# Two-layer decoder step on one core: norm sums, weight loads and cache copies moved at the start, at the layer boundary and ahead of the output projection

## The reference, cut to what matters

```python
def layer(x, lp):                       # 256 prompt tokens and 8 x 4 sample tokens, D = 1024, float32
    xn = rms(x, g_mix)
    q, k, v, xb, gb, gc, cu, cv = split(xn @ w_in)
    ya = dilated window attention of 3 groups of 2 heads (q, k RMS-normed, shared position bias;
         samples attend to the caches), groups weighed by their softmax denominators
    yb = gb * conv3(gc * xb)
    yc = gelu(cu) * (tril(c_ws) @ rms(gelu(cv)) + c_bs)
    h = x + concat(ya, yb, yc) @ w_out
    return h + peer(rms(h, g_ffn))

def peer(xn, wq, k1, k2, eu, ev):       # 8 heads, 16384 experts, top 16 of each head
    q = xn @ wq                          # per head two halves
    e, g = product_key_top16(q, k1, k2)  # 128 expert numbers and gates a token
    hid = gelu(einsum('nd,nhkd->nhk', xn, eu[e]))
    return einsum('nhk,nhkd->nd', g * hid, ev[e])
```

## Time and profile before

| | |
|---|---|
| median of 3 runs | 1879.64 us (1879.1 to 1884.08) |
| profiled execution | 1883.43 us |
| its span, first to last instruction | 1881.7 us |
| busy: PE, DVE, ACT, POOL | 1597.1, 1108.8, 593.0, 681.3 us |
| DMA | 729.73 MB, mean 388 GB/s; q0 (gathers and the caches' loads) 627.43 MB, q1 (SP) 100.48 MB |
| first gather of layer 0 and 1 issued | 222.20 and 1134.31 us |
| mean granted TensorE clock | 0.955 |

### The profile page before, as it was taken

The page is one execution under the profiler, slowest core; times in us unless marked ns, Lnnn a source line. Parts: engine busy times, 40 slices in busy tenths (PEclk is TensorE's granted clock), DMA queues, the critical chain, the costliest instruction groups (busy, mean ns, idle before and its releaser), DMA issues.

```text
span 1881.7 us, 18470 instructions
## 1 busy us (share of the span) xinstructions
PE 1597.1 (85%) x5856; PEld 854.3 (45%) x5856; DVE 1108.8 (59%) x2766; ACT 593.0 (32%) x1854; POOL 681.3 (36%) x672
## 2 busy tenths in 40 slices
PE   6979989998787878777799999999898788777776
PEld 4758955454333333223137897554443333322221
DVE  2233475767877875444444436757778777644444
ACT  2223233333333332222233323323333333322222
POOL 2130134445454534334321103544444544443331
PEclk8889999999899989999999999999998988999999
DMA  5697799999999999999969988999999999999996
GB/s 173 265 395 293 288 379 422 421 421 421 421 421 421 422 421 421 421 422 421 422 251 370 370 332 336 420 421 421 421 421 421 422 421 421 421 422 421 422 421 265
DMA packets 102488, 729.73 MB, mean 388 GB/s; under 512 B 14827, under 2 KB 15925, under 8 KB 21624
## 3 DMA queue, kind: packets, MB, share of 16 engines
q0 software_dynamic: 90112, 627.43, 80.8%
q1 hardware_dynamic: 11732, 100.48, 13.6%
q10 hardware_dynamic: 548, 0.65, 0.1%
HBM read 724.25 MB, written 48.10 MB: 410 GB/s over the span
## 4 chain that ended last, share of the span: by engine, by line
DMA 45%; PE 37%; DVE 10%; ACT 2%; issue 2%; DVEq 1%; POOL 1%; ACTq 1%; SPq 0%; POOLq 0%
DMA arena<-peer_uv,idx 22%; PE bank L1659 18%; DMA wring<-peer_uv,idx 8%; DMA qf<-peer_uv,idx 8%; PE bank L1425 5%; PE bank L1592 4%; PE bank L1623 3%; PE bank L1420 3%; DVE arena L1259 3%; DMA yt<-peer_uv,idx 2%; DMA arena<-cache_keys 2%; DMA arena<-w_out 1%; DVE wring L1259 1%; ACT diag L822 1%; POOL arena L614 1%
## 5 line engine op out<-in xcount | busy, mean ns | idle before, releaser
L1659 PE MATMUL bank<-arena,diag 128*128 128x512 f32 (+1 forms) x1464 | 708.7, 628 | 156.4 <-ACT diag L822 156.2
L614 POOL DMA_INDIRECT arena<-peer_uv,idx x366 | 398.0, 1088 | 654.6 <-PE bank L1659 494.8
L1259 DVE SCALAR_TENSOR_TENSOR arena<-arena,xn 128x1024 f32<-128x1024 f32 x366 | 442.8, 1224 | 295.6 <-DMA arena<-peer_uv,idx 294.1
L1659 PEld LDWEIGHTS bank<-arena,diag 128*128 128x128 f32 (+1 forms) x1464 | 268.4, 190 | 552.4 <-issue 313.1
L814 ACT ACTIVATE act<-hid 128x2 f32<-128x2 f32 x288 | 58.5, 203 | 907.7 <-DVE arena L1259 593.4
L1659 PE MATMUL bank<-wring,diag 128*128 128x512 f32 (+1 forms) x384 | 191.0, 621 | 41.7 <-ACT diag L822 41.7
L822 ACT ACTIVATE diag<-ident,weight 128x128 f32<-128x128 f32 (+1 forms) x576 | 194.7, 385 | 20.1 <-issue 0.3
L1259 DVE SCALAR_TENSOR_TENSOR wring<-wring,xn 128x1024 f32<-128x1024 f32 x96 | 117.4, 1223 | 77.9 <-DMA wring<-peer_uv,idx 76.8
L614 POOL DMA_INDIRECT wring<-peer_uv,idx x96 | 99.3, 1035 | 156.5 <-PE bank L1659 153.1
L817 ACT ACTIVATE weight<-act,gate 128x1 f32<-128x1 f32 x576 | 138.6, 287 | 21.0 <-issue 1.4
L1659 PE MATMUL bank<-qf,diag 128*128 128x512 f32 (+1 forms) x248 | 117.4, 613 | 25.1 <-ACT diag L822 25.1
(11 more groups left out here) (260 smaller groups left out, 1524.0 us busy)
## 6 DMA issues: line engine op xcount, KB each, us to landing
kvs<-cache_a_kv_w SPq DMA_DIRECT2D x32, 1022.0 KB, 10.8
wring<-w_col SPq DMA_DIRECT2D x16, 1024.0 KB, 8.0
wring<-w_tok SPq DMA_DIRECT2D x8, 1408.0 KB, 11.1
arena<-peer_wq SPq DMA_DIRECT2D x10, 1024.0 KB, 20.6
kvs<-cache_a_kv_w SPq DMA_DIRECT2D x16, 508.0 KB, 11.2
arena<-peer_uv,idx POOLq DMA_INDIRECT x366, 21.3
qf<-cache_keys POOLq DMA_DIRECT2D x8, 576.0 KB, 10.4
qf<-cache_values POOLq DMA_DIRECT2D x8, 576.0 KB, 12.2
```

Source lines behind the costliest of these rows:

```text
L614: pool.indirect_dma_start(out=ring[j], out_offset=None, in_=io["peer_uv"], in_offset=bass.IndirectOffsetOnAxis(ap=idx[:, n:n + 1], axis=0) ...
L1259: last = v.scalar_tensor_tensor(out=ring[j][:, 0:D], in0=ring[j][:, 0:D], scalar=1.0, in1=xn[:, i, :], op0=ALU.mult, op1=ALU.mult, accum_o ...
L1659: last = pe.matmul(bank[b0 + half][0:r, :], diag[:, n % 16, 0:r], ring[SLOT_OF[n]][:, D + 512 * half:D + 512 * half + 512], start=False, s ...
```

## The change

- `ms_bank`: the mean of tile 1 goes to bank 3 (before: 1).
- The gains have a semaphore of their own; ACT waits for two loads only and ahead of that does one activation that brings in the square-root table; DVE waits for the gains before its first scaling. In layer 0, PE waits for tile 0 before A0, for tile 1 before A1, and for tile 2 where it did before, ahead of q0.
- Eight shift copies of layer 1 (m = 0 to 7) are issued after SP's small loads, once the first square is done. In layer 1 the copies 8 to 16 follow, one after each of nine loads, then 17 to 23 as before.
- The third quarter of w_out goes to ring slot 4 and is issued ahead of the second, once probt_ps has counted the layer's last transposes of probabilities; query chunk 3, which uses slot 4 later, is issued after 4 and 5, once h_ps has reached 14. Slot 1's first gather does not wait for h_ps. The wait for rows_out stands ahead of query chunk 1.
- `BEFORE_W` is 72: slots 9 and 10 are used up to column 208 in both layers, 11 slots serve the last columns, and layer 1's first two loads are issued from there. A0 and B0 of layer 1 are interleaved with groups 114 to 129, one step k in each.

```diff
-BEFORE_W = 24
+BEFORE_W = 72
...
+        gain_loaded = sem("gain_loaded")
...
-            return bank[(2, 1, 7)[i]]
+            return bank[(2, 3, 7)[i]]
...
-            return (wring[:, 0, 0:KCH * PAIR], ring[0], ring[1], wring[:, 1, 0:KCH * PAIR])[chunk]
+            return (wring[:, 0, 0:KCH * PAIR], ring[0], ring[4], wring[:, 1, 0:KCH * PAIR])[chunk]
...
-            sp.dma_start(gains[:, :, :], io["gain_cols"]).then_inc(x_loaded, 16)
+            sp.dma_start(gains[:, :, :], io["gain_cols"]).then_inc(gain_loaded, 16)
...
+            sp.wait_ge(sq_done, 1)
+            for m in range(8):
+                shift(1, m)
             for l in range(DEPTH):
...
                     load_w(l, c)
-                    for m in range(3 * (c - 2) // 2, 3 * (c - 1) // 2 if c < N_IN else 17):
-                        shift(l, m)
+                    if l == 0:
+                        for m in range(3 * (c - 2) // 2, 3 * (c - 1) // 2 if c < N_IN else 17):
+                            shift(l, m)
+                    elif c < N_IN - 1:
+                        shift(l, c + 6)
+                sp.wait_ge(probt_ps, 3 * (l + 1))
+                load_o(l, 2)
                 sp.wait_ge(pv_done, 2 * (l + 1))
                 load_o(l, 1)
...
                 shift(l, 19)
-                sp.wait_ge(ya_ps, 2 * (l + 1))
-                sp.wait_ge(rows_out, 16 * N_ROWS * (l + 1))
-                load_o(l, 2)
                 sp.wait_ge(in_ps, len(OUTS) * l + IN_DONE[N_IN - 1])
                 load_w(l, N_IN + 1)
+                sp.wait_ge(rows_out, 16 * N_ROWS * (l + 1))
                 sp.wait_ge(h_ps, 16 * l + 1)
                 load_q(l, 1)
                 for m in range(20, 24):
                     shift(l, m)
-                for chunk in range(2, 6):
+                for chunk in (2, 4, 5):
                     load_q(l, chunk)
+                sp.wait_ge(h_ps, 16 * l + 14)
+                load_q(l, 3)
...
-                    elif j == 1:
-                        pool.wait_ge(h_ps, 16 * l + 14)
...
-            a.wait_ge(x_loaded, 48)
             a.wait_ge(set_done, 1)
+            a.activation(warm[:, :], eps[:, :], ACT.Sqrt)
+            a.wait_ge(x_loaded, 32)
...
                 v.drain()
+                if l == 0 and i == 0:
+                    v.wait_ge(gain_loaded, 16)
...
-                    pe.wait_ge(xt_done, 3)
+                    pe.wait_ge(xt_done, 1)
                     out(l, "A0")
                     bias_prompt()
                     out(l, "B0")
                     bias_samples()
                     mix_bias()
+                    pe.wait_ge(xt_done, 2)
                     out(l, "A1")
...
                     if l + 1 < DEPTH:
-                        if n % GROUP and b >= GROUPS_A_LAYER - 8:
-                            if b == GROUPS_A_LAYER - 8:
+                        step = b - TILE_END[1] + 14
+                        if n % GROUP and 0 <= step < 2 * KCH:
+                            if step == 0:
                                 pe.wait_ge(xt_done, 3 * (l + 1) + 1)
-                            if b == GROUPS_A_LAYER - 4:
-                                pe.wait_ge(root_done, 3 * (l + 1) + 2)
-                            step = b - GROUPS_A_LAYER + 8
-                            out(l + 1, "B0" if step >= 4 else "A0", range(step % 4 * 2, step % 4 * 2 + 2))
+                            out(l + 1, "B0" if step >= KCH else "A0", range(step % KCH, step % KCH + 1))
```

## The result

The changed kernel takes 1865.64 us (median, 1864.0 to 1867.95), the kernel before, on the same chip, 1880.67 (1879.1 to 1884.08). The ratio is 0.9919, 95% interval 0.9900 to 0.9937: 15.2 us faster by the ratio, 12 to 19 by its interval. The forecast was 1862.2, and 1865.6 lies inside its range. The profiled executions took 1883.43 before and 1865.96 after, 17.5 us apart, which is the sum of the terms (17.4). That agreement is luck in part, as the trace and the experiments show.

A forecast was written before the change was run, and what follows sets the result against it. DMA at 421 GB/s was taken to bound the gather stages, and PE's chain of waits nearly everywhere outside them. Terms of 8.0 + 3.0 + 2.8 + 2.1 + 1.5 = 17.4 us gave 1862.2 us from the median 1879.64, range 1855.5 to 1871.

The forecast's parts named there:

- the sum of the terms (17.4): Whole kernel: 8.0 + 3.0 + 2.8 + 2.1 + 1.5 = 17.4 us saved; by the bounds 7.3 to 24.
- The bound: Gather stages: DMA at 421 GB/s sets the pace; only savings before a stage or after its last row count, one for one.
- Start, 8.0: Start of layer 0: squares and A0 begin sooner, bias products at 22.6 to 23.2; 8.0 us saved, bounds 3.7 to 11.
- B0 and A1 follow as before: Layer 0, behind the bias products: these products follow unchanged, so the start's 8.0 us carries on.
- The eight copies, 0, with 1.5 for layer 1's projections: Copies at the start cost 0, collision hidden; layer 1's waits before q0 and for BS's weights shrink 1.5 us (0 to 2.7).
- w_out, 3.0 and 2.8: Waits for w_out's third quarter go: layer 0 saves 3.0 us (bounds 1.6, 3.1), layer 1 saves 2.8 (bounds 2.0, 3.9).
- Seam, 2.1: Layer 0's last row to layer 1's transposes: these start at 975.9 in place of 978.0, 2.1 us saved (0 to 3.3).
- The base: Terms taken off the profiled 1883.43 us gave 1866.0; that execution lies 3.8 us above the median 1879.64, hence 1862.2.
- Ring too short: Rival, gather stages: 11 slots for 48 more columns per layer slow landings; 1888 us at 3 us over; 3 in 100.
- A new wait for the old one: Rival: w_out's last or second quarter lands late, layer 1's waits stay; 12 us saved, 1867.6 us; 20 in 100.
- The warmer start: Rival, layer 0's start: products from B0 to B1 also run at the upper clock, 3 to 4 us more, 1858; 12 in 100.
- The gain that does not arrive: Rival: start's gain lost because keys land when they did, some 5 to 8 us less, near 1874; 5 in 100.

The follow-up runs named there:

- e1: The kernel before with the edits of the start alone (gains' own semaphore, square-root table ahead, A0 after the first tile): 1876.22 us, ratio 0.9965.
- e11: The changed kernel with ring slots 5, 11 and 12 left out in both layers (10 slots, 8 in the last 72 columns): 1868.33 us, ratio 0.9926.
- e10: The changed kernel with a quarter of B0 ahead of the bias products and three idle products ahead of each layer's first additions: 1860.43 us, ratio 0.9887.
- e12: The changed kernel with ring slots 3, 4, 5, 11 and 12 left out (8 slots, 6 in the last 72 columns): 1887.69 us, ratio 1.0041.
- e7: The changed kernel with all of B0's projections ahead of the bias products in layer 0: 1864.7 us, ratio 0.9913.
- e2: The kernel before with the eight shift copies moved alone: 1875.44 us, ratio 0.9966.
- e3: The kernel before with the move of w_out's third quarter alone (slot, place on SP, query chunk 3 behind): 1876.01 us, ratio 0.9967.
- e4: The kernel before with the boundary edits alone (slots closed 72 columns early, A0 and B0 in groups 114 to 129): 1881.11 us, ratio 0.9992.
- e9: The changed kernel run again, unedited: 1867.46 us, ratio 0.9923 to the kernel before.
- e5: The kernel before with the eight copies and the w_out move together, neither start nor seam: 1875.74 us, ratio 0.9963.
- e6: The changed kernel with the eight copies put back to layer 1's own time: 1870.94 us, ratio 0.9944 to the kernel before.

## Why the prediction was right, and where its steps were off

- **The bound.** Right. From column 24 to 287 the kernels before, after and e1 to e11 all take 669.5 to 671.3 us, from 324 to 575 632.4 to 633.9, and what a part gains ahead of a stage arrives at the end.
- **Start, 8.0.** Up to the bias products it went as written: squares forecast at 7.0, found at 7.55; A0 16.4 and 16.96; bias products 22.6 to 23.2 and 23.30. A0 ran in 4.98 us, less than the 5.5 put down for the full clock. The step that failed is "B0 and A1 follow as before". In most executions they follow at a lower clock, behind the new wait for the bias rows: in the profiled one 1.94 us are given back in the bias products alone, and 5.6 are left at A1; over the seven executions with this start A1 is 4.0 to 8.3 us earlier than in the five with the old one (54.80 to 55.02). e1 measures 6.6. The Trainium skill (TensorE: Matmul & The Clock Gate, HAM oscillation) says that idle gaps between bursts of products send the array back to its lower clock; its case is one of longer waits, for DMA. I used that rule for A0, which lost its gap, and not for the bias products, which got one. With the gap closed in e10 the clock is 1.00 in place of 0.51, as the rule has it; e12 had the same gap and kept its clock through the bias products, so a gap this short does not bring the fall every time.
- **The eight copies, 0, with 1.5 for layer 1's projections.** The collision is hidden as argued. The 1.5 did not come: the wait before q0 was to shrink by 0.4 from 1.65 and is 1.7 to 2.1 us in the seven kernels that have all the edits (after, e7 to e12). The wait for BS's weights was to go; it stands at 0.7 to 0.9 in three of them, and in the other four a later load waits 0.3 to 1.7 us. In after the two waits sum to 2.43 in place of 2.72. On the other side I did not ask what the emptier queue does for w_out behind them on the same queue. Alone the copies are worth 6.4 us (e2).
- **w_out, 3.0 and 2.8.** Layer 0 gave 2.4 between the two profiled executions (3.05 less 0.65), but these are the extremes: with the third quarter late the wait is 2.2 to 3.05 us in four executions, with it moved 0.6 to 1.8 in ten, 1.4 less on average, below the bound of 1.6. That the last quarter is late next was foreseen. That it would land 2.5 us sooner for the 1 MB less ahead of it was wrong: it landed 12.2 us after its issue in after and 12.2 to 13.3 in the other nine that have the move, against 12.5 to 13.1 in the four without. In layer 1 the time from the first of w_out's products to the first query fell by 3.9 us, 24.43 to 20.52: the wait of 2.03 and 1.9 us more, the slow products behind it among them. That is the bound of 3.9 and above the 2.8; against all three executions that waited for the third quarter with a full queue (22.97 to 24.43) it is 2.5 to 3.9. But that gain is bought twice: e2 has it without the move, and e3 shows the move alone leaving 1.7 us of wait.
- **Seam, 2.1.** 9.29 less 7.24 is 2.05. Right, and within what e4's time could show.
- **The base.** The sum of 17.4 was made against an execution 3.8 us above the median of three runs and then taken off that median. The forecast came out 3.4 us low: 2.4 because the gain over many runs is about 15 and not 17.4 (14.5 by the ratio of e9, the same kernel again), and 1.0 because the median before is 1880.67 with the fourth run. That the two profiled executions lie 17.5 apart is luck in part: the two jumps of the lead, 3.2 won and 2.0 lost, make 1.2 of it. Of the terms, the start is 1.4 too high, the seam 0.6, and w_out and layer 1's projections together 0.3 (7.3 for the 7.0 of e5), each inside the interval of its run. The last of these agrees because terms that failed both ways cancel.
- **Rivals.** Ring too short: fell, e11 prices three slots fewer at 0.9 us, within the noise. A new wait for the old one: half of it came (0.6 us in layer 0 here and up to 1.6 in the other kernels with both edits, 0.7 for w_col in layer 1). The warmer start did not come by itself, but e10 shows that much of it was to be had. The gain that does not arrive: fell, e1 has it and the keys landed 6.2 us earlier.

## What to carry to other kernels

When several edits relieve one queue, ask of each what it is worth once the others are made: here two edits worth 6.4 and 6.2 us alone are worth 7.0 together, each known to within some 2.5 us. After a wait has been moved, look for the gap that it leaves on the tensor engine: a microsecond or two of idle ahead of small products cost itself and, in six executions of seven, the clock of the products right behind it, and a piece of work that was due anyway, put into the gap, won several microseconds back. A single profiled execution differs from another of the same kernel by microseconds at such places, so compare a landmark over all the kernels that share the code. Subtract a sum of terms from the execution that it was read from, and look for what in that execution was chance before carrying it to the median.

## What was not expected of the hardware

- The eight products after a fixed 3.02 us wait take 3.70, 5.2 to 5.4 or 6.6 to 6.75 us from stage to stage of identical code: 5, 15 and 4 of 24 stages. With 2.74 us of idle products inside the wait it was 3.70 four times out of four. The Trainium skill (TensorE: Matmul & The Clock Gate, Part 1: The HAM clock gate) says of the start of a kernel that the count of slow products is run-variable; the 24 stages show the like behind a wait in mid-kernel.
- The 48 small products of the sample bias took 8.48, 9.22 and 13.05 us in three kernels (after, e10, e7), by how much of them fell to the lower clock; 20 us at 0.50 in e7 ate most of what was won ahead of it.
- Six slots, a round of 15 us of DMA, still gave 401 of 421 GB/s from 905 to 935 us.
- w_out's last quarter, 1 MB, landed 12.0 to 13.3 us after its issue in layer 1 while the eight copies stood on the same queue (before, e1, e3, e4, e6), and after 6.8 to 7.6 us with them gone and the third quarter moved.
